# Gate sums on partitions 0, 32 and 64 and one half tile later, set-up loads behind the weights, residual transfers in paced quarters

## What is computed

```python
def run_trunk(x, ...):
    for layer in range(DEPTH):                       # DEPTH = 2
        h = rms_norm(x, g[0])
        if layer % N_MIXERS == 0:
            mix, hr, hi = s5_mixer(h, ...)           # ends with: ag = z @ w_glu
        else:                                        #   a * sigmoid(g)
            mix, C, n, m, cb = mlstm_mixer(h, ...)
        x = x + rms_norm(mix, g[1])
        f, fb = conv_ffn(rms_norm(x, g[2]), ...)
        x = x + rms_norm(f, g[3])

def mlstm_mixer(x, ...):
    up = x @ w_up                                    # [.., 4096]
    xm, z = up[..., :MLSTM_INNER], up[..., MLSTM_INNER:]
    xc_pre, new_buf = causal_dwconv(xm, conv_buf, conv_w, conv_b)
    xc = jax.nn.silu(xc_pre)
    q, k, v = headwise(xc, wq), headwise(xc, wk), headwise(xm, wv)
    gates = (q @ w_gate[:MLSTM_INNER] + k @ w_gate[MLSTM_INNER:2 * MLSTM_INNER]
             + v @ w_gate[2 * MLSTM_INNER:]) + b_gate           # 8 numbers per token
```

## Time and profile before

| | us |
|---|---|
| median of 3 executions | 3983.93 |
| lowest and highest of them | 3980.96, 3985.39 |
| the profiled execution, its own time | 3980.57 |
| its span, first to last instruction | 3978.9 |
| PE busy | 3531.2 (89% of the span) |
| DVE, ACT, POOL busy | 1909.4, 1137.0, 489.9 |
| mean granted TensorE clock | 0.938 of full speed |

### The profile page before, as it was taken

One profiled execution on the slowest core, in us unless ns is written; L12 is line 12 of the kernel. 1 busy time (PEld: TensorE's weight loads), 2 busy tenths in 40 slices (PEclk: granted clock), 3 DMA queues, 4 the chain that ended last, 5 costly groups with the idle time before them and its releaser, 6 DMA issues. The chain is left out here.

```text
span 3978.9 us, 53719 instructions
## 1 busy us (share of the span) xinstructions
PE 3531.2 (89%) x20489; PEld 3262.5 (82%) x20489; DVE 1909.4 (48%) x2968; ACT 1137.0 (29%) x1865; POOL 489.9 (12%) x729
## 2 busy tenths in 40 slices
PE   4549989999999989999459969997995999999997
PEld 4439889999999978999334458887995999999996
DVE  8923445445445562222523346664655454454455
ACT  5223343332233232222123212222113423322321
POOL 2240111010010010000021023222000100000000
PEclk7679999999999999999779979998997999999998
DMA  3554421111111222222179832222103111111112
GB/s 77 141 111 140 127 85 48 43 43 43 38 43 43 74 86 103 99 99 103 27 194 306 293 94 75 83 75 73 43 25 118 38 43 43 43 43 40 41 42 100
DMA packets 365214, 337.09 MB, mean 85 GB/s; under 512 B 42182, under 2 KB 292742, under 8 KB 364866
## 3 DMA queue, kind: packets, MB, share of 16 engines
q1 hardware_dynamic: 345332, 289.11, 23.8%
q0 software_dynamic: 12496, 37.61, 3.5%
q10 hardware_dynamic: 7176, 7.35, 0.6%
HBM read 231.12 MB, written 100.53 MB: 83 GB/s over the span
## 5 line engine op out<-in xcount | busy, mean ns | idle before, releaser
L1579 PE MATMUL pair<-x_head,w_head 128*128 128x384 f32 x1488 | 508.6, 342 | 66.4 <-DVE w_rest L840 38.4
L840 DVE TENSOR_TENSOR w_rest<-w_raw,w_head 128x1024 fp32r<-128x1024 f32 x228 | 282.0, 1237 | 469.0 <-ACT w_head L836 468.9
L1579 PE MATMUL pair<-x_rest,w_head 128*128 128x384 f32 x1488 | 505.5, 340 | 0.0
L1579 PE MATMUL pair<-x_head,w_rest 128*128 128x384 f32 x1488 | 505.1, 339 | 0.0
L836 ACT ACTIVATE w_head<-w_raw 128x1024 fp32r<-128x1024 f32 x228 | 242.6, 1064 | 742.6 <-PE pair L856 194.6
L1238 PE MATMUL pair<-x_head,w_head 128*128 128x384 f32 x1056 | 354.2, 335 | 10.2 <-DVE w_rest L840 7.6
L1238 PE MATMUL pair<-x_rest,w_head 128*128 128x384 f32 x1056 | 353.6, 335 | 0.0
L1238 PE MATMUL pair<-x_head,w_rest 128*128 128x384 f32 x1056 | 353.6, 335 | 0.0
L1579 PEld LDWEIGHTS pair<-x_head,w_head 128*128 128x128 f32 x1488 | 285.8, 192 | 72.3 <-issue 63.0
L1579 PEld LDWEIGHTS pair<-x_rest,w_head 128*128 128x128 f32 x1488 | 285.8, 192 | 0.0
L1579 PEld LDWEIGHTS pair<-x_head,w_rest 128*128 128x128 f32 x1488 | 285.6, 192 | 0.0
(11 more groups left out here) (501 smaller groups left out, 6919.7 us busy)
## 6 DMA issues: line engine op xcount, KB each, us to landing
w_raw<-in_ffn_w_up_dram SPq DMA_DIRECT2D x88, 512.0 KB, 3.8
out_dram<-hs SPq DMA_DIRECT2D x64, 512.0 KB, 7.0
w_raw<-in_s_w_glu_dram SPq DMA_DIRECT2D x48, 512.0 KB, 4.1
w_raw<-in_ffn_w_down_dram SPq DMA_DIRECT2D x44, 512.0 KB, 3.7
hs<-in_state_mlstm_C_dram SPq DMA_DIRECT2D x44, 512.0 KB, 5.9
w_raw<-in_mlstm_w_up_dram SPq DMA_DIRECT2D x32, 512.0 KB, 4.3
f<-in_state_mlstm_C_dram SPq DMA_DIRECT2D x40, 256.0 KB
xm_d<-xm SPq DMA_DIRECT2D x16, 576.0 KB, 3.9
```

The lines of the kernel that those rows point to most:

```text
L840: dve.tensor_tensor(self.rest[slot][:, :], self.raw[slot][:, :], self.head[slot][:, :].bitcast(F32), ALU.subtract).then_inc(self.split, 1)
L1579: m = pe.matmul(out[:, 0:TB], lhs[slot][:, P * k:P * k + P], rhs[:, k, TB * c:TB * c + TB], start=(k == 0 and q == 0), stop=(k == KD - 1 a ...
```

## The change

Four edits, all in `front` and its classes.

1. **Gate sums.** The three accumulators move to three different strips of partitions: block 0 to bank 6 partitions 0 to 7, block 1 to bank 7 partitions 32 to 39, block 2 to bank 6 partitions 64 to 71. The six matmuls of tile j - 1 now stand between half 0 and half 1 of tile j; those of the last tile stand alone at the end. Their number and size stay.
2. **Set-up loads.** stack is loaded after the weight loads of step 1, m_stack after those of step 2, c after those of step 3. The transposes on PE and the copies on DVE move from step 2 to step 5, `folded` from step 4 to step 6.
3. **Quarters.** Every load and store of a residual block becomes four DMAs of two channel tiles each. A store's quarter k waits only for its own renewal.
4. **Pace.** In the Glu stage quarter k of a transfer also waits on POOL for a step: the load of block 0 for steps 5 to 8, of block 1 for 9 to 12, the store of block 0 for 13 to 16, the load of block 2 for 17 to 20, the store of block 1 for 21 to 24 (`glu.free`). The store of block 2 and all transfers of norm2 are not paced.

```diff
...
-    def load(self, eng, c):
-        eng.dma_start(self.x[c][:, :, :], self.rows_of(c)).then_inc(self.x_in[c], 16)
-
-    def store(self, eng, c):
-        eng.wait_ge(self.renewed, self.HALF * (c + 1))
-        eng.dma_start(self.rows_of(c), self.x[c][:, :, :]).then_inc(self.stored[c], 16)
+    def load(self, eng, c, k):
+        eng.dma_start(self.x[c][:, 2 * k:2 * k + 2, :], self.rows_of(c)[:, 2 * k:2 * k + 2, :]).then_inc(self.x_in[c], 16)
+
+    def store(self, eng, c, k):
+        eng.wait_ge(self.renewed, self.HALF * c + k + 1)
+        eng.dma_start(self.rows_of(c)[:, 2 * k:2 * k + 2, :], self.x[c][:, 2 * k:2 * k + 2, :]).then_inc(self.stored[c], 16)
...
-        self.acc = [env.bank[6][0:2 * HEADS, 0:TB], env.bank[7][0:2 * HEADS, 0:TB], env.bank[6][32:32 + 2 * HEADS, 0:TB]]
+        self.acc = [env.bank[6 + c % 2][32 * c:32 * c + 2 * HEADS, 0:TB] for c in range(NB)]
...
                 up_tile(pe, self.env, n, 0, self.x_head, self.x_rest, banks[0])
+                gates(j - 1, 1 - p_)
                 pe.wait_ge(self.zed, j)
                 up_tile(pe, self.env, n + 1, 1, self.x_head, self.x_rest, banks[1])
+
+        def gates(j, p_):
+            first, last = isinstance(j, int) and j == 0, isinstance(j, int) and j == IT - 1
             pe.wait_ge(self.filled, j + 1)
             pe.wait_ge(self.silued, j + 1)
             for k, x in ((0, self.xc), (1, self.xm)):
...
         self.tiles(pe, body)
+        gates(IT - 1, (IT - 1) % 2)
...
-            glu.sync(sp, 0)
-            ready.sync(sp)
-            for k in range(1, steps):
+            for k in range(steps):
                 glu.sync(sp, k)
+                if k == 1:
+                    ready.stacks(sp)
+                if k == 2:
+                    ready.m_stacks(sp)
+                if k == 3:
+                    ready.cells(sp)
...
-            norm1.load(pool, 0)
-            norm1.load(pool, 1)
-            norm1.store(pool, 0)
+            def paced(move, c, first):
+
+                for k in range(KD // 2):
+                    pool.wait_ge(glu.free, min(first + k, steps))
+                    move(pool, c, k)
+
+            paced(norm1.load, 0, 5)
+            paced(norm1.load, 1, 9)
+            paced(norm1.store, 0, 13)
             for k in range(KD // 2):
                 norm1.rest(pool, 0, k)
-            pool.wait_ge(norm1.stored[0], 16)
-            norm1.load(pool, 2)
-            norm1.store(pool, 1)
+            pool.wait_ge(norm1.stored[0], 16 * (KD // 2))
+            paced(norm1.load, 2, 17)
+            paced(norm1.store, 1, 21)
             for k in range(KD // 2):
                 norm1.rest(pool, 1, k)
-            norm1.store(pool, 2)
+            for k in range(KD // 2):
+                norm1.store(pool, 2, k)
...
-                if k == 2:
+                if k == 5:
                     ready.tensor(pe)
```

More of the change, by code:

```diff
@@ L1477, in scale @@
             if r == 0:
[L1478 removed]
+                dve.wait_ge(self.x_in[c], 16 * self.HALF)
         def renew(k):
@@ L1512, in __init__, with stacks @@
             "stack_in", "m_in", "c_in", "g_in", "turned", "done", "formed"))
-    def sync(self, sp):
+    def stacks(self, sp):
         i, r = self.i, 0
@@ L2123, in _ @@
             pool.wait_ge(ffn_.headed, 2 * FBLOCKS)
-            norm2.load(pool, 1)
-            norm2.store(pool, 0)
+            for k in range(KD // 2):
+                norm2.load(pool, 1, k)
+            for k in range(KD // 2):
+                norm2.store(pool, 0, k)
             for k in range(KD // 2):
                 norm2.rest(pool, 0, k)
-            pool.wait_ge(norm2.stored[0], 16)
-            norm2.load(pool, 2)
-            norm2.store(pool, 1)
-            norm2.store(pool, 2)
-            pool.wait_ge(norm2.stored[1], 16)
+            pool.wait_ge(norm2.stored[0], whole)
+            for k in range(KD // 2):
+                norm2.load(pool, 2, k)
+            for c in (1, 2):
+                for k in range(KD // 2):
+                    norm2.store(pool, c, k)
+            pool.wait_ge(norm2.stored[1], whole)
             pool.wait_ge(norm2.headed, 3 * (KD // 2))
             up.pool(pool)
-            pool.wait_ge(norm2.stored[2], 16)
+            pool.wait_ge(norm2.stored[2], 16 * (KD // 2))
         @block.tensor
@@ L2244, in _ @@
             norm2.heads(act, 2, 0, 4)
-            act.wait_ge(norm2.stored[1], 16)
+            act.wait_ge(norm2.stored[1], 16 * (KD // 2))
             up.scalar(act)
@@ L2260, in _ @@
                 glu.vector(dve, k)
-                if k == 2:
+                if k == 5:
                     ready.vector(dve)
-                if k == 4:
+                if k == 6:
                     ready.folded(dve)
```

19 lines of the change are left out of this document (11 added, 8 removed).

## The result

The changed kernel takes **3933.38 us** (median of 4 executions, 3930.30 to 3943.29) beside 3984.66 us of the kernel before in the same comparison (4 executions, 3980.96 to 3986.18). The ratio is 0.9872, with a 95% interval of 0.9857 to 0.9887: 51.3 us less. The forecast was 3927.5, which is 56.4 less than before, with a range of 3920 to 3945. The time lies in the range; the forecast gained 5 us too much.

The account below looks back on a forecast made before the run. PE was taken to bound the kernel, busy 3531.2 of 3978.9 us; gains 13.0 + 12.7 + 1.5 + 29.2 = 56.4 gave 3924.2 from the profiled execution, 3927.5 on the median of 3983.93; range 3920 to 3945.

Parts of the forecast that it names:

- 1. Set-up loads: Start of Glu: PE's gap of 10.99 us before 301.18 and 2.0 of slow clock go; gain 13.0 us.
- The rival in which the 15.30 us move along: Glu, loads of c: wk's stall moves with them, 12.7 us come back, total 3940; chance 0.09.
- 2. Quarters and their pace: Glu: three PE gaps at whole residual transfers go, 7.9 us, with 4.8 of slow clock; gain 12.7 us.
- 3. The gap at 460.20: Glu: DVE's split, held up by POOL's `rest` of block 0, runs free; between 2.3 and -1.5, taken as 1.5 us.
- 4. Gate sums on three strips: Up: all three blocks' passes in flight, four turns; 1.29 us a tile, 18.1 for tiles 1 to 14, 0.3 for the last.
- the rival of seven turns: Up, gate sums: passes start in order, seven turns instead of four, 14.6 us less gain, total 3942; chance 0.12.
- draining: Up, gate sums: each change between strips drains PE, 7.6 us a tile, slower at 4020; chance 0.03.
- 5. Half a tile later: Start of Up: PE no longer waits for silu of tile 0; 12.4 - 1.5 = 10.8 us gained with the entry.
- 6.: norm2's residual transfers in quarters: no PE gap is put down to them; gain nothing.

Follow-up runs that it names:

- e2_setup: Kernel before with only the set-up loads moved behind the weight loads of steps 1 to 3, transposes and copies three steps later: 3972.31 us, ratio 0.9969.
- e12_cells_first: Kernel of e2_setup with the three loads of c back ahead of the weight loads of step 1, only the stacks moved: 3971.77 us (one execution).
- e4_spread: Changed kernel with the four `rest` of block 0 one behind each of steps 17 to 20, each followed by a load quarter of block 2: 3925.21 us, 0.9854.
- e9_spread: The kernel of e4_spread measured again with more rounds, against the kernel before: 3928.00 us, ratio 0.9851.
- e10_spread_unpaced: Kernel of e9_spread without the paced waits of loads and stores; `rest` of block 0 stays one a step: 3927.49 us, ratio 0.9853.
- e7_unpaced: Changed kernel without the waits that let POOL issue one quarter a step in Glu: 3928.06 us, ratio 0.9869 to the kernel before.
- e5_strips: Kernel before with one line changed: block c's gate sums start at partition 32c, their place in the order unchanged: 3966.33 us, ratio 0.9966.
- e6_late: Kernel before with the gate sums half a tile later, on the old partitions: 3970.59 us, ratio 0.9966.
- e11_inter: Kernel of e9_spread without the wait for a step between the `rest` of block 0, only one load quarter issued between two: 3928.74 us, ratio 0.9848.

## Why the prediction was right, and where it was wrong

**1. Set-up loads.** Right, with the size a little low: 13.0 forecast, 15.2 measured in A (e2_setup), 13.5 of it at the place. The three issues of c took 2.79 + 0.57 + 1.14 = 4.5 us where I had asked for under 4, and PE did not wait. Of the 2.2 us above the forecast 1.7 are the clock that happened not to fall behind a gap. The rival in which the 15.30 us move along is out. e12_cells_first shows the larger part of the reason: without the stacks ahead the three issues took 7.8 us less. Another 4 us came with the later place, for a reason that no run takes apart.

**2. Quarters and their pace.** The three gaps went, as forecast, and weight loads beside a quarter landed in up to 6.0 us. The two paced kernels without the lock-out, e4_spread and e9_spread, have an A 13.5 us shorter than e2_setup, where the steps 2 and 3 together forecast 14.2. But the gain is that of quarters which stand apart, and for the stores DVE's work sets them apart: the pace, whose arithmetic I left with the quarters', is worth 0 to 1 us (e10_spread_unpaced). Where four quarters did go out together, in e7_unpaced and e10_spread_unpaced, a weight load was as late as beside a whole transfer (8.4 and 8.5 us), and a slow clock and the sums of the norms hid it.

**3. The gap at 460.20.** This is the step that failed. It said that with the `rest` behind the quarter of step 16 "this split runs free" and that the next ones "may meet POOL in its place; between 2.3 and -1.5 I take 1.5". They met, and for 7.45 us, not for one `rest` more. The sum there is 0.78 + 5.34 of idle time and 2.1 of slow clock, against 2.32 before: -5.9 instead of +1.5. These 7.4 us are a little more than the whole miss in A and B, 6.9. The bound was wrong, not only the choice: -1.5 was taken from the earlier trace rows, where a split met the last of the `rest`, as if a meeting could cost no more than one instruction. All four stand in the same queue with nothing between them, so the far bound was their sum: POOL's 3.63 for two, 7.3 for four, less the time that PE's queued product covers. The pace is what made it so. Before, the four `rest` came in two pairs, with a wait for ACT's heads between them; behind a store quarter that waits for step 16 all four were ready, and came together, right after DVE's step, which is when the next split begins.

By the Trainium skill, "SBUF — State Buffer", section "Who interferes with whom", a DVE instruction with two SBUF inputs and a GpSimd instruction that reads SBUF exclude each other for a whole instruction, and the one that comes second waits. The traces agree in kind (7.45 us with four `rest`, 2.76 with the last of two, and 2.65 for a `rest` behind a split), but a lock for one instruction would have let the split in after 1.1 us at 446.65, and it came in only behind the fourth. Between the two `rest` of a pair a waiting split did get in, 15 times of 15, as a lock for one instruction would have it.

**4. Gate sums on three strips.** Right: 18.1 + 0.3 forecast, and 19.5 in e5_strips, which holds also the 1.3 us of tile 0's sums that the forecast has in part 5; so 18.2. Against the rival of seven turns stand the sums of 1.40 us, and against draining as well.

**5. Half a tile later.** 10.8 forecast, 9.5 in e6_late, and with the 1.3 of tile 0 it is 10.8. L856 follows the last product after 0.27 us. Of the 12.4 us 2.9 are not saved with the old strips, since the sums of tile 0 have to be made all the same. The two steps together are 29.0 for 29.2.

**6.** norm2's quarters: nothing was seen of them. The stretch between A and B, in which norm2 runs, is 936.99 us before and 936.35 after.

**The sum.** A and B give 20.6 + 29.0 = 49.5 (from 20.57 and 28.96) of the 51.3. The difference to the forecast, 56.4 - 49.5 = 6.9, is part 3's 7.4, with 0.5 of the other sign in the rest. That the medians miss by 5.1 only is luck in part: the stretches outside A and B scatter by more than the difference.

**A better version.** e9_spread is the fastest of the paced ones, 3928.00 and in its first measurement 3925.21; e10_spread_unpaced, without the pace, is as fast at 3927.49. So a small edit was worth more than the whole pace: a wait that puts a step between two `rest`, with one load quarter behind each.

## What to carry to other kernels

When a queue's instructions are held back by a new wait, ask not only who is late, but what is then released all at once, and bound a meeting with it by the whole burst. Small transfers help when they stand apart: sent together they make a load as late as the whole does. Where their producer already spaces them, a pace on top of it adds only a risk. Measure the stretch between two fixed points of the program when the rest scatters by more than the edit is worth.

## What the runs showed of the hardware

- Four POOL instructions of 1.8 us, one behind the other, kept a DVE instruction with two SBUF inputs out for 6.4 us; the same happened at the end of Glu in the six kernels whose `rest` of block 1 wait for step 24 (8.23 to 8.26 us for a split of 1.22, and 2.73 to 2.75 in the other eight, where it meets only the last `rest` of a pair). A pause of 2.1 us on POOL let it in; of three DMA issues of 0.7 us that it met in e11_inter, only the last did. A split that came 0.2 us before the end of the first of two `rest` got in between them (1.30 us).
- The issue of one load of small elements stood 15.30 us with eight stacks ahead of it in the queue and 4.08 without them (with the like loads before and behind it 16.77 and 8.96), 3.67 (e2_setup) and 2.79 (changed kernel) three steps later, and 1.32 on an unloaded queue.
- Plain fp32 matmuls with eight output rows, on three strips, ran beside each other at no cost that could be seen: the twelve passes took four turns, 1.40 us, where eight of them on one strip and four on a second had taken eight, 2.68 us.
- A weight load of 512 KB, 4.1 us on its own (the median), landed after 8.4 to 9.1 us beside a whole transfer of 1.5 MB, after 5.6 to 6.0 beside a quarter of it, and after 7.7 to 8.5 beside four quarters sent together.
- Gaps of equal length are not equally dear: behind 2.67 us at 411.47 in e2_setup the clock stayed at 1.00, behind 2.64 us at 424.60 before it was at 0.50 for three us.
